# A joined change in the second mixer: its compression is projected with each head once and its network stands between query tiles, and turns stand in front of products in rounds with an even slot

## What is computed

```
def nsa_mixer(h, w_in, b_gate, q_g, k_g, cmp_pos, cmp_w1, cmp_w2, rel_table, w_out):
    q, kc, vc, ks, vs, kw, vw, gl = jnp.split(h @ w_in, splits, axis=-1)   # 1024, then 6 x 256, then 48 columns
    q = rms_norm(q.reshape(B, S, G, J, Dh), q_g)                           # G = 4 groups, J = 4 heads, Dh = 64
    gates = jax.nn.sigmoid(gl + b_gate)
    starts = jnp.arange(n_cmp) * 16                                        # n_cmp = 15 windows of 32 rows
    def compress(a, pos, w1, w2):
        blk = a[:, tok] + pos[:, None, :]                                  # windows of one head's keys or values
        return jax.nn.gelu(blk.reshape(..., 32 * Dh) @ w1) @ w2
    Kc = rms_norm(compress(kc, cmp_pos[0], cmp_w1[0], cmp_w2[0]), k_g[0])
    Vc = compress(vc, cmp_pos[1], cmp_w1[1], cmp_w2[1])
    p_c = masked_softmax(q @ Kc * scale + bias)                            # compressed attention
    ...                                                                    # selected and window attention
    return (gates0 * o_c + gates1 * o_s + gates2 * o_w) @ w_out
```

## Time and profile before

| | |
|---|---|
| time, median of 3 runs | 3226.84 us (3224.78 to 3228.95) |
| profiled execution | 3224.55 us |
| its span | 3222.7 us |
| TensorE busy | 98% |
| VectorE busy | 79% |
| ScalarE busy | 52% |
| GpSimd busy | 14% |
| read from memory | 577 MB, 179 GB/s over the span |

### The profile page before, as it was taken

How to read it: one execution, slowest core, us unless ns; L and a number is a source line. 1 busy time by engine, 2 the same in 40 slices (tenths; PEclk the granted TensorE clock), 3 DMA queues, 4 the chain that set the end, 5 groups by cost and what they waited for, 6 DMA issues and landing times.

```text
span 3222.7 us, 52953 instructions
## 1 busy us (share of the span) xinstructions
PE 3165.0 (98%) x20423; PEld 2739.3 (85%) x20423; DVE 2533.0 (79%) x4365; ACT 1689.3 (52%) x2704; POOL 465.9 (14%) x317
## 2 busy tenths in 40 slices
PE   7999999999999899999999999999999999999999
PEld 7799977888888679987788888889978888898787
DVE  7789989888878569999977667758767677687775
ACT  3454555544455455555545555446664454566543
POOL 0268000000000357500000000001240000022300
PEclk9999999999999999999999999999999999999999
DMA  9545455577756225545566555555335555544355
GB/s 344 175 138 181 142 164 171 204 266 251 261 200 248 79 81 175 166 146 170 170 208 223 188 190 178 187 175 181 125 125 187 191 180 190 176 150 144 131 190 170
DMA packets 160889, 582.01 MB, mean 181 GB/s; under 512 B 18432, under 2 KB 20224, under 8 KB 160640
## 3 DMA queue, kind: packets, MB, share of 16 engines
q1 hardware_dynamic: 156528, 569.70, 52.8%
q10 hardware_dynamic: 3600, 8.35, 0.7%
q0 software_dynamic: 512, 0.57, 0.1%
HBM read 576.97 MB, written 1.05 MB: 179 GB/s over the span
## 4 chain that ended last, share of the span: by engine, by line
PE 91%; DVE 5%; issue 1%; ACT 1%; POOL 1%; DMA 1%; SPq 0%; ACTq 0%; DVEq 0%
PE P L2119 22%; PE P L892 17%; PE P L955 12%; PE P L2096 11%; PE P L895 9%; PE P L881 8%; PE P L2082 2%; DVE LOW L537 1%; PE P L860 1%; PE P L919 1%; PE P L794 1%; PE P L863 1%; DVE ACC L647 1%; PE P L1137 1%; PE P L1151 0%
## 5 line engine op out<-in xcount | busy, mean ns | idle before, releaser
L537 DVE TENSOR_TENSOR LOW<-RING,HI 128x1024 fp32r<-128x1024 f32 x884 | 1083.1, 1228 | 152.9 <-ACT HI L524 152.5
L524 ACT ACTIVATE HI<-RING 128x1024 fp32r<-128x1024 f32 x988 | 1036.0, 1051 | 251.6 <-DMA RING<-in_fdB 58.0
L892 PE MATMUL P<-HT,HI 128*128 128x512 f32 x2368 | 591.0, 392 | 0.0
L892 PEld LDWEIGHTS P<-HT,HI 128*128 128x128 f32 x2368 | 433.5, 188 | 83.6 <-issue 1.0
L895 PEld LDWEIGHTS P<-HT,LOW 128*128 128x128 f32 x2368 | 323.1, 190 | 23.1
L895 PE MATMUL P<-HT,LOW 128*128 128x256 f32 x2368 | 330.2, 282 | 0.0
L2096 PE MATMUL P<-HT,HI 128*128 128x256 f32 x2048 | 282.4, 286 | 0.0
L537 POOL TENSOR_TENSOR LOW<-RING,HI 128x1024 fp32r<-128x1024 f32 x104 | 252.0, 2429 | 91.4 <-ACT HI L524 80.3
L2096 PEld LDWEIGHTS P<-HT,HI 128*128 128x128 f32 x2048 | 258.7, 192 | 0.1
L881 PE MATMUL P<-HT,HI 128*128 128x256 f32 x1792 | 241.8, 288 | 0.5 <-ACT HI L524 0.5
L881 PEld LDWEIGHTS P<-HT,HI 128*128 128x128 f32 x1792 | 223.9, 192 | 10.9 <-issue 5.1
(11 more groups left out here) (439 smaller groups left out, 5364.3 us busy)
## 6 DMA issues: line engine op xcount, KB each, us to landing
RING<-in_pu SPq DMA_DIRECT2D x256, 512.0 KB, 3.3
RING<-in_pv SPq DMA_DIRECT2D x256, 512.0 KB, 3.3
RING<-in_fgA SPq DMA_DIRECT2D x44, 512.0 KB, 3.3
RING<-in_fuA SPq DMA_DIRECT2D x44, 512.0 KB, 3.3
RING<-in_fdA SPq DMA_DIRECT2D x44, 512.0 KB, 3.2
RING<-in_fgB SPq DMA_DIRECT2D x44, 512.0 KB, 4.1
RING<-in_fuB SPq DMA_DIRECT2D x44, 512.0 KB, 3.5
RING<-in_fdB SPq DMA_DIRECT2D x44, 512.0 KB, 4.2
```

Source lines behind the costliest of these rows:

```text
L524: act.activation(c.his[i % NHL], c.raw[m % NR], ACT.Copy).then_inc(*c.hi.at(("hi", m)))
L537: eng.tensor_tensor(c.low[m % NR], c.raw[m % NR], c.his[i % NHL].bitcast(F32), ALU.subtract).then_inc(*sig.at(("lo", m)))
L892: pe.matmul(ps, hi[:, k * 128:k * 128 + 128], c.both[:, :, k, :], start=k == 0, stop=False)
```

## The change

It does two things. First, an nsac tile now holds the columns of two heads, once each, and there are 4 of them. VectorE makes the windows of both heads from one product, 4 operations a tile, with source and target on different halves of the partitions where they must; the position table is laid out for that. The nsaw1 tiles move in the stream behind nsaq 1 and nsaq 2. The compression network is cut up: the turns of the gates stand behind nsaq 0, the first hidden rows behind nsaq 1, key rows and the second hidden rows behind nsaq 2, the key sums behind nsaq 3, value rows behind nsak 1. Compressed scores of group g stand one value tile earlier, those of group 0 behind nsak 3. The modulation's piece 8 and the tables of bias are spread over other tiles. Second, `turns_first` (new) makes the turns stand in front of the products in rounds from the third on whose even item has a slot and whose odd item has none.

```diff
@@ -107,7 +107,7 @@
...
-    c["pos"] = i["odd_cmp_pos"][0].reshape(2, 16, 2, 64).transpose(2, 3, 0, 1).reshape(128, 32)
+    c["pos"] = np.tile(i["odd_cmp_pos"][0].reshape(2, 16, 2, 64).transpose(3, 2, 0, 1).reshape(64, 64), (2, 1))
@@ -164,8 +164,7 @@
...
-    kv = w[:, 1024:1536].reshape(1024, 8, 1, 64)
-    a["nsac"] = stationary(np.tile(kv, (1, 1, 2, 1)).reshape(1024, 1024))
+    a["nsac"] = stationary(w[:, 1024:1536])
@@ -293,8 +292,9 @@
...
     if s == "mix1":
-        order = [("nsac", j) for j in range(8)] + [("nsag", 0)] + [("nsaq", j) for j in range(8)]
-        order += [("nsak", j) for j in range(4)] + [("nsaw1", 0), ("nsaw1", 1)] + [("nsav", j) for j in range(4)]
+        order = [("nsac", j) for j in range(4)] + [("nsag", 0), ("nsaq", 0), ("nsaq", 1), ("nsaw1", 0), ("nsaq", 2)]
+        order += [("nsaw1", 1)] + [("nsaq", j) for j in range(3, 8)]
+        order += [("nsak", j) for j in range(4)] + [("nsav", j) for j in range(4)]
         order += [("nsao", k) for k in list(NSA_SLOTS[0].values()) + NSA_SLOTS[1]]
         return [(t, "dve") for t in order]
@@ -348,7 +348,8 @@
...
-    spread(todo, [(("nsac", j), 1) for j in range(4, 8)] + [(("nsaq", j), 1) for j in (0, 1, 2, 3, 4, 6)])
+    spread(todo, [(("nsac", 3), 1), (("nsag", 0), 1)] + [(("nsaq", j), 1) for j in (0, 1, 2, 3, 4, 6)]
+           + [(("nsak", j), 1) for j in range(2)])
@@ -1162,6 +1163,11 @@
...
+def turns_first(a, m):
+
+    return m >= 2 and 2 * m in a.slots[0] and 2 * m + 1 not in a.slots[0]
+
+
 def attention_tensor(pe, c, a, scores, closing=None, extra=None):
     a.slots_done = 0
     for m in range(a.items // 2):
@@ -1172,11 +1178,13 @@
             extra(m)
         if 2 * m in a.slots[0]:
             attention_slot(pe, c, a, a.slots[0][2 * m])
-        if m >= 2:
+        if m >= 2 and not turns_first(a, m):
             attention_products(pe, c, a, m - 2, closing)
         if m >= 1:
             attention_turn(pe, c, a, 2 * m - 2)
             attention_turn(pe, c, a, 2 * m - 1)
+        if turns_first(a, m):
+            attention_products(pe, c, a, m - 2, closing)
         if 2 * m + 1 in a.slots[0]:
             attention_slot(pe, c, a, a.slots[0][2 * m + 1])
@@ -1247,7 +1255,7 @@
...
-        if m >= 2:
+        if m >= 2 and not turns_first(a, m):
...
+        if turns_first(a, m):
+            attention_heads_scalar(act, c, a, m - 2)
@@ -1668,21 +1679,84 @@
...
-    for j in range(8):
+    for j in range(4):
         if j >= 2:
             project(pe, c, "nsac", j)
...
+    modulation_tensor(pe, c, ("nsag", 0))
...
+    def gates_turned():
+        ps = open_bank(pe, c, s, "gates")
+        pe.wait_ge(*c.by(s, "sigmoids"))
+        for t in range(2):
...
+    def hidden(kv):
+        n = c.place["nsaw1", kv]
+        w = c.raw[n % NR]
+        ps = open_bank(pe, c, s, "hidden", kv)
+        pe.wait_ge(*c.landing(n))
+        pe.wait_ge(*c.by(s, "windows", 2 * kv + 1))
+        for l in range(16):
+            m = pe.matmul(ps[0:64, 0:60], w[:, l * 64:l * 64 + 64], f.z[kv][:, l * 60:l * 60 + 60], start=l == 0,
+                          stop=l == 15)
+        m.then_inc(*c.pe.at(("used", n), (s, "hidden", kv)))
...
+    def key_rows():
+        ps = open_bank(pe, c, s, "kc")
+        pe.wait_ge(*c.by(s, "gelu", 0))
...
+    def key_row_sums():
+        ps = open_bank(pe, c, s, "kc_sums")
+        pe.wait_ge(*c.by(s, "kc_squares"))
...
+    def value_rows():
+        ps = open_bank(pe, c, s, "vc")
+        pe.wait_ge(*c.by(s, "repeated"))
...
+    def compressed(g):
+        if g == 0:
+            pe.wait_ge(*c.by(s, "kc_normed"))
+        pe.wait_ge(*c.by("normed", "nsaq", 2 * g + 1))
...
     for j in range(8):
         project(pe, c, "nsaq", j)
         if j:
             heads_sums(pe, c, "nsaq", j - 1, f.sq[(j - 1) % 2], f.pack("bd64"))
+        if j == 0:
+            gates_turned()
+        if j == 1:
+            hidden(0)
+        if j == 2:
+            key_rows()
+            hidden(1)
+        if j == 3:
+            key_row_sums()
         if j == 6:
             heads_rows(pe, c, "nsaq", 0, f.rr[0], f.pack("hsel"))
         modulation_tensor(pe, c, ("nsaq", j))
@@ -1692,61 +1766,23 @@
             heads_sums(pe, c, "nsak", j - 1, f.sq[(j - 1) % 2], f.pack("bd64"))
         else:
             heads_sums(pe, c, "nsaq", 7, f.sq[1], f.pack("bd64"))
+        if j == 1:
+            value_rows()
         if j == 2:
             heads_rows(pe, c, "nsaq", 1, f.rr[1], f.pack("hsel"))
...
+        if j == 3:
+            compressed(0)
+        modulation_tensor(pe, c, ("nsak", j))
...
+    def after(s4):
+        if s4 == 0:
             heads_sums(pe, c, "nsak", 3, f.sq[1], f.pack("bd64"))
...
+        if s4 == 1:
+            heads_rows(pe, c, "nsak", 0, f.rr[0], f.pack("hsel"))
+        if s4:
+            turned(s4 - 1)
+        if s4 < 3:
+            compressed(s4 + 1)
@@ -1795,15 +1831,31 @@
...
+    for j in range(4):
         feed(act, c, "act", "nsac", j)
-        if j in (4, 6):
-            bias_rows(j // 2 - 2)
+        if j in (1, 3):
+            bias_rows(j // 2)
         modulation_scalar(act, c, ("nsac", j), f.gate)
...
+        if j == 1:
+            feed(act, c, "act", "nsaw1", 0)
+            gelu(0)
+        if j == 2:
+            feed(act, c, "act", "nsaw1", 1)
+            act.wait_ge(*c.by(s, "kc"))
+            act.activation(f.kc[:, 0:60], c.psum(s, "kc")[:, 0:60], ACT.Copy, scale=-1.0).then_inc(
+                *c.act.at((s, "kc_copied")))
+            act.activation(f.kc_sq, c.psum(s, "kc")[:, 0:60], ACT.Square).then_inc(
+                *c.act.at((s, "kc_squares"), ("free", s, "kc")))
+            gelu(1)
+        if j == 4:
+            act.wait_ge(*c.by(s, "kc_means"))
+            act.activation(f.kc_rr, f.kc_rr, ACT.Sqrt).then_inc(*c.act.at((s, "kc_root")))
         modulation_scalar(act, c, ("nsaq", j), f.gate)
...
+        modulation_scalar(act, c, ("nsak", j), f.gate)
     for g in range(4):
         feed(act, c, "act", "nsav", g)
+        if g == 0:
+            act.wait_ge(*c.by("heads_rows", "nsaq", 0, 1))
+            heads_root_scalar(act, c, "nsak", 0, f.rr[0], f.pack("eps"))
+        exps(g)
         if g:
             turned(act, g - 1)
-        exps(g)
@@ -1868,78 +1911,29 @@
...
-    for j in range(8):
+    for j in range(4):
         feed(dve, c, "dve", "nsac", j)
-        kv, g = divmod(j, 4)
+        kv = j // 2
         zz = f.z[kv].rearrange("p (l g n) -> p l g n", l=16, g=4)
         dve.wait_ge(*c.by("product", "nsac", j))
-        for par in range(2):
-            pp = slice(64 * par, 64 * par + 64)
-            po = f.pack("pos")[:, 16 * kv:16 * kv + 16][pp, :].unsqueeze(2).broadcast_to([64, 16, 15])
-            m = dve.tensor_tensor(zz[pp, :, g, :], strided_window(c.psum("nsac", j)[:, 0:256], pp, par), po, ALU.add)
+        for half in range(2):
+            src, g = slice(64 * half, 64 * half + 64), 2 * (j % 2) + half
+            for par in range(2):
+                po = f.pack("pos")[:, 32 * par + 16 * kv:32 * par + 16 * kv + 16][src, :].unsqueeze(2).broadcast_to(
+                    [64, 16, 15])
+                m = dve.tensor_tensor(zz[64 * par:64 * par + 64, :, g, :],
+                                      strided_window(c.psum("nsac", j)[:, 0:256], src, par), po, ALU.add)
         m.then_inc(*c.dve.at((s, "windows", j), ("free", "nsac", j)))
         modulation_vector(dve, c, ("nsac", j))
     feed(dve, c, "dve", "nsag", 0)
-    dve.wait_ge(*c.by(s, "gates_turned"))
-    for t in range(2):
-        m = dve.tensor_copy(f.g3[:, t, :], c.psum(s, "gates")[:, t * 64:t * 64 + 48])
-    m.then_inc(*c.dve.at((s, "gates"), ("free", s, "gates")))
+    modulation_vector(dve, c, ("nsag", 0))
...
+    dve.wait_ge(*c.by(s, "tables"))
+    dve.wait_ge(*c.by(s, "masks"))
+    for j in range(8):
+        feed(dve, c, "dve", "nsaq", j)
+        if j % 2 == 0:
+            dve.wait_ge(*c.by(s, "toep", j // 2))
+        if j == 5:
+            heads_inverse_vector(dve, c, "nsaq", 0, f.rr[0])
+        if j == 7:
+            normed(0)
+        tb = f.tb[:, 2 * j:2 * j + 2, :]
+        dve.scalar_tensor_tensor(out=tb, in0=tb, scalar=-1.0, in1=f.causal.unsqueeze(1).broadcast_to([128, 2, 384]),
+                                 op0=ALU.mult, op1=ALU.add).then_inc(*c.dve.at((s, "bias", j)))
+        if j == 1:
+            dve.wait_ge(*c.by(s, "gates_turned"))
+            for t in range(2):
+                m = dve.tensor_copy(f.g3[:, t, :], c.psum(s, "gates")[:, t * 64:t * 64 + 48])
+            m.then_inc(*c.dve.at((s, "gates"), ("free", s, "gates")))
+        if j == 4:
+            key_row_means()
+            repeated()
+        if j == 6:
+            key_rows()
+        modulation_vector(dve, c, ("nsaq", j))
+    for j in range(4):
+        feed(dve, c, "dve", "nsak", j)
+        if j == 1:
+            heads_inverse_vector(dve, c, "nsaq", 1, f.rr[1])
+        if j == 2:
+            value_rows()
+        if j == 3:
+            normed(1)
```

(13 more changed lines are left out.)

220 lines of the change are left out of this document (83 added, 137 removed).

## The result

The changed kernel took **3205.7 us** (median of four runs, 3205.19 to 3206.93), the kernel before 3227.45 us in the same comparison (3224.78 to 3228.95): a ratio of 0.9936, 95% interval 0.9924 to 0.9947, a gain of 21.7 us (17 to 25 by the interval). The forecast was 3208.6 us, 18.2 us of gain, with a range of 3203.0 to 3215.0. The profiled execution took 3206.93 us with a span of 3205.1 us.

What follows compares the result with a forecast made beforehand. It took TensorE, busy 91% of the span, to bound the kernel. Its terms, 11.5 + 1.2 - 0.6 - 2.7 - 1.6 + 5.1 - 0.2 + 2.0 + 3.5 = 18.2 us, gave 3208.6 us, range 3203.0 to 3215.0.

Steps and rivals of the forecast that it cites:

- Four tiles less, and the waits at the gates: Projections: four compression tiles of 2.88 us go, 11.5 us; waits of 0.51 and 0.65 us go, together 1.2 us.
- The windows: Compression tiles: doubled window operations on VectorE delay the LOW halves, a loss of 0.6 us, bounds 0.3 and 1.3.
- The supply: Third query tile lands late: 2.7 us wait before the first head sums, then 1.6 us of low clock.
- The network: Compression network spread between query tiles: of 9.0 us, waits and slow clock go, a gain of 5.1 us.
- the value rows' bank: Third key tile waits for the bank VectorE frees from the value rows: 0.2 us lost, bounds 0 and 1.
- the start of the attention: Compressed scores run one group ahead, so the 2.00 us wait for shares goes: 2.0 us, bounds 0 and 3.
- Turns in front of products: Attention rounds: two-round periods of 8.50 and 8.65 us instead of 9.16; six patterns gain 3.5 us, bounds 0 and 4.0.
- the supply holds: Rival: the third query tile lands before 1001.8, so its wait and low clock go; 3204.3 us, chance 0.26.
- the rounds give nothing: Rival: waits in the rounds and at the attention's start only move; 3214.1 us, chance 0.11.
- supply late more than once: Rival: two more query tiles 3 us late, costing 6 to 9 us with the clock; 3215 to 3218, chance 0.10.
- the drain: Rival: ScalarE's gelu comes 1.4 us later than its table load allows, delaying the key rows; 3210.0 us, chance 0.02.
- slower: Rival: late supply at every query tile, 4 us for eight tiles, 32 us against 22.5 gained; 3236 us, chance 0.02.

Runs made afterwards that it cites:

- tables_spread_alone: Changed kernel with the second to fourth bias table issued behind other query tiles and VectorE's operations on them one per tile: stage 181.85 us, kernel 3206.51 us.
- experiment 5: No new kernel: clock windows of tables_spread_alone read against other profiles; low clock after 0.21 us idle in a dense stretch, costing 1.6 us.
- rounds_alone: Kernel before with only the turns put in front of products in rounds with an even slot: 3223.15 us against 3226.61, ratio 0.9987.
- compression_alone: Changed kernel with products in front of turns everywhere, as before: stage 185.48 us, kernel 3208.62 us against 3226.61, ratio 0.9943.
- before_again: The kernel before, unchanged and profiled a second time: 3227.05 us, stage 202.15 us.

## Why the prediction was right

**Four tiles less, and the waits at the gates: right, with one wrong place.** The first piece gained 12.83 us, 12.6 without the turns of the gates that moved out of it, for 12.1. But the 0.51 us of the earlier trace rows did not stand in front of the gates' tile, as I wrote. Counted from the start of the projections, that row is the last compression tile, whose own transfer was late; the gates' tile is the row behind. It went with its tile in either case.

**The windows: right, a bit dear.** TensorE waits 0.67 us for the LOW half of the third tile instead of 0.37, and that half lasts 1.23 us, the lower case. The next two tiles are 2.96 and 2.94 us apart, not 2.88. That makes 0.30 + 0.14 = 0.44 us for the 0.6 I took.

**The supply: the mechanism right, the 0.1 us luck.** The wait was 2.67 us for 2.7, but 2.32 and 2.18 in two more profiles. I had the third query tile land near 1004.5, though the terms named give 1002.9 + 1.9 = 1004.8, and a wait of 3.0. With this profile's later start they are 1007.65 and 1007.95; its HI half started at 1007.30. TensorE was ready for the sums at 1006.38, 0.3 us sooner than forecast too, and so the two misses cancel. That the tables are what holds it is shown by tables_spread_alone. Its clock cost 0.41 + 0.90 = 1.3 us, for 1.6. What I had not seen is that two queues stand behind that transfer, so that turning one around gives nothing.

**The network, the value rows' bank, the start of the attention: right.** From the first head sums to the turn of the last shares 5.23 us went, for -1.6 + 5.1 - 0.2 + 2.0 = 5.3. The closeness is in part luck. The forecast's own terms for the network, 9.0 - 2.08 - 1.9, give 5.0 and not 5.1, and from start to start its pieces cost 3.65 us now for 9.08 before, a gain of 5.4. The clock cost 0.3 us less than assumed. Against that stands a cost that no term names: the compressed scores behind the third value tile, split by the wait of 0.20 us (experiment 5), take 2.25 us (1069.28 to 1071.53), the next ones 1.47. The bank made no wait. No wait over 0.5 us stands between the first head sums and the attention. Where 2.00 us stood in the earlier trace rows, 0.45 are left. The 0.32 us that the fourth piece lost lie between the first turned weights and the first slot: 11.08 us (1084.16 to 1095.24), 10.57 before, and 11.08 or 11.09 in rounds_alone and compression_alone too. I didn't follow it further, and its cause is open.

**Turns in front of products: right, under-sized.** I followed two patterns and got 8.50 and 8.65 us, with 0.22 us of wait surviving in every second. Behind the first slot it is in no pattern; the periods are all 8.48 us. The gain is the upper bound of 0.67 us a pattern, 4.0 us instead of 3.5. rounds_alone has the same 8.48 us without the new compression, and compression_alone, without the turns in front, 9.17 us.

**What was missing: the low clock behind the rounds.** The last piece gained 2.55 us. 0.6 us is the sixth pattern, and 2.0 us is low clock that both profiles of the kernel before have and the changed kernel has not: 1.6 us at the closing products (5.03 us from 1165.00 to 1170.03, now 3.44) and 1.0 us at the norm's turns, less 0.6 us by which the wait for VectorE in front of these turns grew (1.96 to 2.58). I had read the clock at the network and nowhere behind it. This is nearly the whole difference of 20.5 to 18.2 us. Nothing in the rows says when it comes, so I see no way to have forecast it.

The rivals: *the supply holds* is refuted by the wait, *the rounds give nothing* by the periods, *supply late more than once* by the rows without waits at the later tiles, *the drain* by the gelu's row, and *slower* by the same rows: one long wait, and none at the six query tiles behind it.

## What to carry to other kernels

When a wait stands behind a transfer, look for every queue behind it before you turn one around: here ScalarE's square, VectorE's copy out of a bank and the gelu each took the wait over, and only less traffic in front of the tile (one table of 0.79 MB, 2.4 us) removed it. Work that you take off one engine's late stretch must be spread as thinly where you put it; two operations a tile on VectorE brought a wait of 2.07 us, nearly what the other had been (2.67). And measure a local change inside the profile, between two rows of the stage: that repeated within 0.3 us in the two kernels profiled twice, where executions of one kernel scatter by 0.6 to 8.5 us.

## What the runs showed of the chip

The granted clock fell in places that the waits alone don't explain. Behind the same waits in the network, the low level lasted until before 1068 us in the kernel before and past 1075 us in rounds_alone, some 4 us of difference. In a stretch with TensorE busy for 3.79 of 4 us it fell in two profiles of eleven that have that stretch, for 1.6 us. At the closing turns TensorE was busy for 1.69 of 3 us in before_again and 1.68 of 3 us in compression_alone; behind that the granted clock was 0.54 in the first and 1.00 in the second. Nor was a longer wait the worse one: in front of the norm's turns TensorE waited 1.96 us in the kernel before, with low clock behind it, and 2.58 us with the change, with full clock. Where a kernel was profiled twice (the kernel before and the changed one), the low stretches behind the last slot came or stayed away alike in both. Single losses of 1 to 4 us of this kind are thus as large as the effects of single edits, and two kernels that differ by less should be compared by their waits. What decides when the clock falls stays open.
